# A two-layer sequence model on one core: first products run ahead of four phase barriers, and squares and splits handed between engines

## The reference, cut to what matters

```python
xn = rms_norm(h, mix_pre_g)
proj = xn @ w_in                                  # z, xbc, dt, q, k, v
y_ssd = ssd_mixer(z, xbc, dt_raw, ...)            # Mamba-2, gated by silu(z), then rms_norm
y_sb = rms_norm(stick_breaking_attention(q, k, v).reshape(B, L, 1024), sb_norm_g)
mix = jnp.concatenate([y_ssd, y_sb], axis=-1) @ w_out
h = h + rms_norm(mix, mix_post_g)
xn = rms_norm(h, ffn_pre_g)
gu = xn @ w_up
g = causal_dwconv(gu[..., :D_FF], ffn_conv_w, ffn_conv_b)
f = (gelu(g, approximate=True) * gu[..., D_FF:]) @ w_down
h = h + rms_norm(f, ffn_post_g)
```

## Time and profile before

| | us |
|---|---|
| median of 3 runs (lowest, highest) | 2510.24 (2506.31, 2510.31) |
| the profiled execution: its own time | 2508.72 |
| the profiled execution: span from first to last instruction | 2507.0 |
| PE busy in it | 2399.7 (96%) |
| DVE busy | 1348.2 (54%) |
| ACT busy | 962.7 (38%) |
| POOL busy | 996.3 (40%) |

### The profile page before, as it was taken

One profiled execution on the slowest core, in us unless ns is written; L12 is line 12 of the kernel. 1 busy time (PEld: TensorE's weight loads), 2 busy tenths in 40 slices (PEclk: granted clock), 3 DMA queues, 4 the chain that ended last, 5 costly groups with the idle time before them and its releaser, 6 DMA issues. The chain is left out here.

```text
span 2507.0 us, 45147 instructions
## 1 busy us (share of the span) xinstructions
PE 2399.7 (96%) x18588; PEld 1535.4 (61%) x18588; DVE 1348.2 (54%) x1427; ACT 962.7 (38%) x1695; POOL 996.3 (40%) x744
## 2 busy tenths in 40 slices
PE   8999979999999998999999999999999999989997
PEld 5666655666666665665666666445854445578856
DVE  7767964334344436475444444325677847235544
ACT  3227855555555555342111111224554422223321
POOL 4446667555566555003444444100035443101160
PEclk9999989999999999999999999999999999999999
DMA  3122210000000001221111111332623541133411
GB/s 121 51 85 76 85 34 26 18 26 26 18 27 25 19 18 51 90 88 42 50 50 50 50 50 50 101 99 87 214 86 102 159 143 43 59 89 89 151 56 68
DMA packets 108567, 173.90 MB, mean 69 GB/s; under 512 B 26273, under 2 KB 76641, under 8 KB 106993
## 3 DMA queue, kind: packets, MB, share of 16 engines
q1 hardware_dynamic: 108400, 171.55, 21.6%
HBM read 145.77 MB, written 25.76 MB: 68 GB/s over the span
## 5 line engine op out<-in xcount | busy, mean ns | idle before, releaser
L1387 DVE TENSOR_TENSOR_SCAN att_kept<-att_keep 128x143 f32<-128x143 f32 (+7 forms) x128 | 174.8, 1373 | 319.3 <-ACT att_keep L1303 312.8
L218 PE MATMUL ps<-x_lo,whi_z 128*128 128x342 f16 x1008 | 310.8, 308 | 0.0
L217 PE MATMUL ps<-x_hi,whi_z 128*128 128x342 f16 x1008 | 310.3, 308 | 0.2 <-POOL wlo_z L191 0.2
L219 PE MATMUL ps<-x_hi,wlo_z 128*128 128x342 f16 x1008 | 309.9, 307 | 0.0
L1134 POOL TENSOR_TENSOR att_beta<-att_beta,att_kept 128x256 f32<-128x256 f32 (+7 forms) x128 | 197.5, 1543 | 220.3 <-DVE att_kept L1387 201.1
L1180 PE MATMUL ps<-x_hi,whi_z 128*128 128x348 f16 x576 | 180.8, 314 | 14.1 <-PEq L607 14.1
L2444 PE MATMUL ps<-second_x_hi,whi_z 128*128 128x512 f16 (+1 forms) x480 | 179.6, 374 | 3.4 <-POOL wlo_z L2413 1.9
L1182 PE MATMUL ps<-x_hi,wlo_z 128*128 128x348 f16 x576 | 180.4, 313 | 0.0
L1181 PE MATMUL ps<-x_lo,whi_z 128*128 128x348 f16 x576 | 180.3, 313 | 0.0
L2445 PE MATMUL ps<-second_x_lo,whi_z 128*128 128x512 f16 (+1 forms) x480 | 179.2, 373 | 0.0
L2446 PE MATMUL ps<-second_x_hi,wlo_z 128*128 128x512 f16 (+1 forms) x480 | 179.2, 373 | 0.0
(11 more groups left out here) (582 smaller groups left out, 6088.2 us busy)
## 6 DMA issues: line engine op xcount, KB each, us to landing
wraw_z<-in_w_up SPq DMA_DIRECT2D x44, 512.0 KB, 3.5
wraw_z<-in_w_second SPq DMA_DIRECT2D x30, 512.0 KB, 3.6
wraw_z<-in_w_qkv SPq DMA_DIRECT2D x24, 512.0 KB, 3.5
wraw_z<-in_w_down SPq DMA_DIRECT2D x20, 512.0 KB, 3.6
raw_down<-in_w_down SPq DMA_DIRECT2D x20, 512.0 KB, 4.1
seg<-dt_a_sums SPq DMA_DIRECT2D x18, 512.0 KB, 5.4
second_work<-parked_units SPq DMA_DIRECT2D x7, 1280.0 KB, 6.4
wraw_xbc<-in_w_in SPq DMA_DIRECT2D x13, 512.0 KB, 3.5
```

Source lines behind the costliest of these rows:

```text
L217: nc.tensor.matmul(out, hi, xhi, start=(k == 0), stop=False)
L218: nc.tensor.matmul(out, hi, xlo, start=False, stop=False)
L219: return nc.tensor.matmul(out, lo, xhi, start=False, stop=(k == L.parts * L.kb - 1))
L1387: nc.vector.tensor_tensor_scan(out[:, 1:t.keys], x, x, 1.0, ALU.mult, ALU.min).then_inc(s_scan, 1)
```

## The change

- **SSD to attention.** POOL cuts the first attention weight block between `keep_x` and `add_x` of the last chunk, not after them. PE makes groups 0 and 1 of the attention projection (48 matmuls) at the end of the SSD block, into banks 0 and 1; the sums stay there, and attention starts with group 2.
- **Attention to out projection.** The squares of pairs 0 to 6 and their sums are made on DVE inside attention (7 squares and 6 adds, at query blocks 4 and 5 of the next pair); only block 7 is left to ACT and DVE in the out phase. The sum of squares (`mixed_squares`) is allocated earlier for that; the square is put in `rs_ssd_y`, which is free by then.
- **Low parts of the attention norm.** `by_vector(k)` is now `k % 2 == 1`: DVE makes four of eight low parts, POOL four. The cut of weight load 3 (`high(3)`, `low(3)`) moves behind them.
- **Out projection to feed-forward.** The first 24 matmuls of `w_up` (block 0, tile 0) are made at the end of the out block.
- **Feed-forward to down projection.** The first 24 matmuls of the down projection (512 columns, 8 feature blocks) are made at the end of the up block.

```diff
 def by_vector(k):
-    return k % 4 == 3
+    return k % 2 == 1
...
+QKV_AHEAD = 2
...
                         for g in range(2):
                             keep_x(c, g)
+                        if c == NCH - 1:
+                            pool.wait_ge(s_lin, NT * (DB - 1))
+                            cut_first(nc, S, pool, Lq, 1)
                         for g in range(2):
                             add_x(c, g)
...
-                for s in range(SLOTS):
-                    pool.wait_ge(s_lin, NT * (DB - SLOTS + s + 1))
-                    cut_first(nc, S, pool, Lq, s + 1)
+                pool.wait_ge(s_lin, NT * DB)
+                cut_first(nc, S, pool, Lq)
...
+                pe.wait_ge(Lq.cut, 1)
+                for g in range(QKV_AHEAD):
+                    pe.wait_ge(s_out, Z_GROUPS - QKV_AHEAD + g + 1)
+                    for j in range(DB):
...
+                        nc.tensor.matmul(lin_ps(g), hi, xhi, start=(j == 0), stop=False)
+                        nc.tensor.matmul(lin_ps(g), hi, xlo, start=False, stop=False)
+                        nc.tensor.matmul(lin_ps(g), lo, xhi, start=False, stop=(j == DB - 1))
...
-                for g in range(GROUPS):
+                nc.tensor.sem_inc(s_lin, QKV_AHEAD)
+                for g in range(QKV_AHEAD, GROUPS):
                     linear(g, 0, DB)
...
+                def square(p):
+                    x = S.z[:, p, F0:T]
+                    dve.wait_ge(s_o, NSTEP * (p + 1))
...
+                    nc.vector.tensor_tensor(zsq if p else zacc, x, x, ALU.mult).then_inc(s_zsq, 1)
+                def add_square(p):
...
+                    nc.vector.tensor_tensor(zacc, zacc, zsq, ALU.add).then_inc(s_zacc, 1)
                 for s in range(STEPS):
                     for a in range(2):
                         scan(s, a)
+                    p = ATT[s].p - 1
+                    if p >= 0 and ATT[s].j == 4:
+                        square(p)
+                    if p >= 1 and ATT[s].j == 5:
+                        add_square(p)
...
                 for y in OUT_PARTS:
                     part(y)
                     if y.use == 0:
-                        pe.wait_ge(s_zacc, DB - 1)
+                        pe.wait_ge(s_zacc, 1)
...
+                pe.wait_ge(Lu.cut, 1)
+                pe.wait_ge(C.low, DB)
+                pe.wait_ge(s_sq, max(u for u in range(len(OUT_UNITS)) if unit_bank(u) == 0) + 1)
+                for j in range(DB):
+                    up_product(nc, S, Lu, 0, 0, j)
...
-                for k in range(DB):
-                    if k >= 3:
-                        act.wait_ge(s_zacc, k - 2)
-                    nc.scalar.activation(sqz[(k - 1) % 2] if k else acc[:, :], S.z[:, k, F0:T], ACT.Square).then_inc(s_zsq, 1)
-                    if k in (5, 7):
-                        high(k // 2)
+                nc.scalar.activation(sqz, S.z[:, DB - 1, F0:T], ACT.Square).then_inc(s_zsq, 1)
+                high(2)
...
                 cut_by_scalar(nc, act, N)
+                high(3)
                 high(4)
...
-                for k in range(1, DB):
-                    dve.wait_ge(s_zsq, k + 1)
-                    if k >= 2:
-                        dve.wait_ge(s_zacc, k - 1)
-                    nc.vector.tensor_tensor(acc[:, :], acc[:, :], sqz[(k - 1) % 2], ALU.add).then_inc(s_zacc, 1)
-                    if k in (5, 7):
-                        low(k // 2)
+                dve.wait_ge(s_zsq, 1)
+                nc.vector.tensor_tensor(acc[:, :], acc[:, :], sqz, ALU.add).then_inc(s_zacc, 1)
+                low(2)
                 dve.wait_ge(s_zroot, 1)
                 cut_by_vector(nc, S, dve, N)
+                low(3)
                 low(4)
...
                 for s in range(SLOTS):
                     pe.wait_ge(L.emptied, s + 1)
                     pe.wait_ge(L.cut, s + 1)
-                    for n in range(NT - 1):
+                    for n in range(s == 0, NT - 1):
...
                 products(nc, pe, L, normed(S), lambda s: psum_tn(S, s), SLOTS, 2 * FFB, NT, FT, F0)
+                k0, k1 = DOWN_PARTS[0]
+                pe.wait_ge(Ld.cut, 1)
+                pe.wait_ge(L.emptied, 2 * FFB + 1)
+                pe.wait_ge(s_lo, 2 * k1)
+                for k in range(k0, k1):
...
+                    nc.tensor.matmul(out, hi, fhi, start=(k == 0), stop=False)
...
+                nc.tensor.sem_inc(s_pr, 1)
                 for u in range(len(DOWN_UNITS)):
...
-                    part(u, 0)
+                    if u:
+                        part(u, 0)
```

49 lines of the change are left out of this document (33 added, 16 removed).

## The result

| | before | changed |
|---|---|---|
| median (lowest to highest) | 2510.24 (2506.31 to 2511.03, 5 runs) | 2495.14 (2493.0 to 2501.25, 5 runs) |
| ratio of the medians, 95% interval | | 0.9944 (0.9931 to 0.9958) |
| the profiled execution: time, span | 2508.72, 2507.0 | 2498.35, 2496.6 |

The change is 15 us faster. Two later measurements of the same two kernels gave 0.9935 (0.9922 to 0.9948) and 0.9938 (0.9921 to 0.9954). Over all runs of this study the mean is 2510.8 for the kernel before (54 runs) and 2495.9 for the changed one (14 runs), each with a scatter of some 2.4 us. The forecast was 2498 (2492 to 2504).

What follows compares the result with a forecast made beforehand. PE, busy 96% of the span, bounds the kernel; time lies only where it waits or runs slowly. Gains 3.2 + 0 + 6.5 + 1.7 + 0.5 = 11.9 us off 2508.7, plus 1.5 for the median, give 2498 (2492 to 2504).

Steps and rivals of the forecast that it cites:

- SSD to attention: First barrier: POOL's moved cut opens it 3.7 us earlier; with 0.3 gained and 0.8 given back, 3.2 us.
- the slow sums: Start of attention: PE's six sums, after about 3 us of waiting, run slower and give back 0.8 us.
- the 48 products: End of SSD block: PE's attention matmuls take 7.1 us beside POOL's cut and cost nothing.
- Squares: Inside attention: DVE's 13 added instructions, 17 us in all, fit its idle time waiting for ACT; cost 0.
- The rival by which the kernel would get slower: Attention: DVE's 13 instructions delay POOL, then PE; 2515 at 1.3 us each, 2523.7 at 1.95; chance 0.03.
- Attention to out: Out block: sums and first `out_y` earlier, 3.8 us, plus shorter low parts, 2.7 us; 6.5 us together.
- The chain term: Out block: with one square and add left, sums follow the 72 matmuls unbroken; first `out_y` 3.8 us earlier.
- The second term: Low parts of the attention norm: DVE's 12 instructions beside POOL's 4 take 20.2 us, not 22.9; 2.7 us less.
- The absolute sums: Low parts under the skill's port rule: lists simply add, 25.2 us before and 23.5 now, 1.7 us less.
- Out to up: Third barrier: 24 matmuls fill 3.5 of 3.75 us idle; second sum starts 2.35 us earlier but slower; 1.7 us.
- Up to down: Fourth barrier: PE arrives last, about 1 us late, waits 4 us for weight load 1; 0.5 us gained.
- the clock stays up: Attention, second sum of the mix and down: shorter idles, fewer restarts; 15 us gained, 2495; chance 0.10.

Runs made afterwards that it cites:

- the second trace: Profile of the changed kernel unchanged, measured again against the kernel before: 2494.64 us, 0.9935.
- squares_four: Changed kernel, but DVE makes each of the seven squares inside attention four times: 2499.89 us, 0.9960 of the kernel before.
- down_five: Changed kernel, but 15 instead of 24 down-projection matmuls ahead of the fourth barrier, nine behind it: 2496.05 us, 0.9936 of the kernel before.
- the third: Profile of the changed kernel unchanged, measured a third time against the kernel before: 2495.08 us, 0.9938.
- squares_only: Kernel before plus only the squares of seven pairs and their sums on DVE inside attention: 2507.76 us, 0.9988.
- split_only: Kernel before with only the low parts re-shared, DVE making four of eight and POOL four: 2510.56 us, 0.9998.
- b1_only: Kernel before plus only the first-barrier change, POOL's moved cut and 48 attention matmuls ahead: 2509.22 us, 0.9993.
- cut_only: Kernel before plus only POOL's first cut moved ahead of the adds, without the 48 products: 2508.56 us, 0.9991.

## Why the prediction was right, and where it was not

The time lies in the range, 3 us below the value forecast; "faster" came true.

**SSD to attention (3.2 forecast; 3.1, 1.3, 3.0).** The moved cut did what was worked out: last cut at 336.35, forecast 335.7, which is 3.5 us earlier counted from the last chunk product (3.7 forecast). Two terms behind it were mis-sized. DVE's adds ended 3.1 us earlier and not 4.0 (1.4 in the second trace), and the slow sums cost 1.8 us and not 0.8: they took 3.85 us in place of 2.02, at half the clock. So the exponential came 1.3 us earlier in the first trace and 0.45 later in the second, where 3.2 were forecast. What made up for it was not foreseen: PE, slow for 6.8 us there, waited only 1.89 us for POOL's meta weights and not 3.07, and no slow stretch followed, which is the other 1.7 of the 3.1 us. That the sum of this interval came out at 3.1 is luck: with the same code up to there, `squares_four` and `down_five` gained 1.9 and 0.4. I had priced the 48 products at nothing. The runs without them put their price at 2.5 to 4.2 us at the exponential, and 0.7 to 2.5 of it at the ninth step.

**Squares (0; 0.1, 0.0, 0.1).** Right, and `squares_four` gives a measure of the cover: it is larger than the idle time on which the forecast rested. The rival by which the kernel would get slower was far off; it needed 0.92 us per instruction on PE.

**Attention to out (3.8 + 2.7; 3.0 or 5.1, then 3.0).** The chain term is right: 3.0 us earlier and sums of 1.9 in place of 2.87 make 4.0; the rest of the difference is slow stretches in the last steps of attention. The second term (2.7) was mis-sized and came out nearly right by a part that I left out. DVE's list took 21.3 us, not 20.2. Its twelve instructions, which overlap by 0.1 us each, cover 20.2 us, just as summed; what the sum left out is the 1.12 us in which DVE waits for ACT's last high part. That idle stands in the earlier trace rows too, but there POOL ended last and it cost nothing. So 1.6 us are gained. How the two engines meet can be read instruction by instruction: POOL's low part starts at 978.60 and ends at 981.68, and DVE's, begun at 979.75, ends at 982.77, 1.1 us behind it. In the traces of before and after every DVE instruction of the list that starts while one of POOL's runs ends 1.1 us behind that one, and every low part of POOL's that starts while one of DVE's runs ends 1.9 to 2.0 us behind that one. The Trainium skill ("SBUF — State Buffer", section "Who interferes with whom") calls the port pair that the two share an exclusive lock; the forecast worked out 1.7 us from that. The trace agrees with the lock and with the difference. The absolute sums, 25.2 and 23.5 us, are 2.3 and 2.1 above the 22.9 and 21.3 measured, because a turn costs 1.1 and 1.9 us there and not 1.25 and 2.12. The other 1.4 us are PE's clock, which fell behind the old wait of 3.9 us and stays up behind three short ones.

**Out to up (1.7; 2.0, 2.0, 1.4).** Right, but for the size of the slow sum: 0.45 us of idle at the first sum, 2.42 ahead of the second (2.5 forecast), which took 0.84 us in the first two traces (up to 1.48 forecast) and 1.51 in the third. The clock fell there or in the wait of 2.84 us for a low part just behind it, a wait that the kernel before has too. Taking the products out again costs 1.4 to 2.05.

**Up to down (0.5; 0.9, 2.4, 0.7).** Right in mechanism: PE is last at the barrier by 1.2 us (1 forecast), and waits 3.93 us for weight load 1 (4 forecast). What it gains depends on whether the clock falls.

**Where the other 3 us are.** The sum of the terms was 11.9, the traces give 12.1 to 13.8. Further, the profiled execution of before was a short one, 2508.7 against a mean of 2510.8; the forecast allowed 1.5 us for that. With the mean gain of the three spans (12.6) this makes 14.7 of the 14.9 us between the means of all runs. It is bookkeeping and not a cause: no trace shows where the longer executions of before spend those 2 us. The rival "the clock stays up" (2495) gave the time, but not by its own terms. Of its three places the clock fell at the sums of the SSD norm and around the second sum of the mix, and stayed up at down in one trace of three; it also stays up behind the low parts, which the rival did not name.

**What stays open.** Up to the last matmul the profiles count 17 to 23 pieces of 3.4 us at half the clock for before and the single parts, and 11 to 19 for the changed kernel and its variants. Part of that difference lies in the second layer, which no kernel touches. Whether this is chance or an effect of when that layer starts was not tried. The gains of `squares_only`, `split_only`, `b1_only` and `cut_only`, 3.0, 0.2, 1.6 and 2.2 us in median, and the 4.7 of the up products, were measured with a scatter of 2 to 3 us per run, so their sum says nothing finer about the whole. Not tried: to place the sums of the SSD norm behind group 3 or 4, or to let ACT empty group 0 ahead of its squares, so that PE keeps work while ACT and DVE sum.

## What to carry to other kernels

Work moved ahead of a barrier pays only if PE would otherwise stand still there and has something else to cover the next wait: the 24 up matmuls filled an idle of 3.75 us and gained 1.4 to 2, while the 48 attention matmuls took away what PE had to do while ACT and DVE summed squares. Put as much ahead as the gap holds, not a whole unit: 15 matmuls left two waits of 1.4 us, 24 left one of 3.9, and the interval became 1.0 to 2.6 us shorter (a gain that the medians do not show). In the first layer, from the first attention step on, PE kept its clock at every wait up to 2.1 us. At waits of 2.8 us and more the clock was at half during or right behind them, but for three cases (3.76, 3.92 and 3.93 us); so there cutting a wait in two was worth more than its length. This is no rule for other code: in the second layer, among small matmuls, the clock also fell at waits of 2.0 us and less, and stayed up at one of 2.6.

## What the runs showed of the hardware that was not expected

- An engine off the path set another's pace through a buffer: PE done with group 2 a microsecond earlier (its clock was back at full 2 us sooner) gave POOL its weight buffer earlier, and POOL's cut of 2.99 us then stretched DVE's seven adds from 10.64 to 12.37 us.
- The same wait in the same code does not always cost the clock: behind the 3.93 us at the down projection it fell in two of three executions of the changed kernel (15.8 and 16.0 us for the interval, 14.4 where it stayed up), and around the 2.42 us at the second sum and the 2.84 us behind it it was low for 6.8, 6.8 and 10.3 us.
- The clock was also at half where PE was at work nearly throughout: 9.36 us of the 10.3 from 2213.5 on, with 88 small matmuls (the profile models the ends of matmuls). In the 6.8 us ahead of that PE was busy for 5.1 at the full clock.
- DVE's squares in attention cost POOL 10% on its products beside them (217.4 us in place of 197.5, for 128 instructions each; 217.7 in `squares_only`), and PE nothing. With four times as many squares it was 213.8, so this cost does not grow with their number.
- DVE and POOL took turns in the low parts: in the two traces that were read instruction by instruction, whichever started second ended 1.1 us (DVE) or 1.9 to 2.0 us (POOL) behind the first, alone they take 1.2 to 1.3 and, for POOL's weight cut, 2.12.
